# Gate and up products of the FFN: two of eight k-tile pairs by Strassen's scheme, with eight PSUM banks

## The reference, cut to what matters

```
x = x + mixer(rmsnorm(x))
h = rmsnorm(x, ffn_norm[i])
x = x + (silu(h @ w_gate[i]) * (h @ w_up[i])) @ w_down[i]
```

## Time and profile before

| | |
|---|---|
| median of 3 runs | 2175.33 us (2174.98 to 2175.91) |
| the profiled execution | 2175.17 us, span 2173.3 us |
| TensorE busy / weight loads | 2158.6 us (99%) / 1796.3 us (83%) |
| VectorE busy | 1162.3 us (53%) |
| ScalarE busy | 979.9 us (45%) |
| DMA moved | 401.57 MB, mean 185 GB/s |
| slots of the two FFN first halves | 2 x 11 x 16 = 352 of 748 |

### The profile page before, as it was taken

How to read it: one execution, slowest core, us unless ns; L and a number is a source line. 1 busy time by engine, 2 the same in 40 slices (tenths; PEclk the granted TensorE clock), 3 DMA queues, 4 the chain that set the end, 5 groups by cost and what they waited for, 6 DMA issues and landing times.

```text
span 2173.3 us, 27329 instructions
## 1 busy us (share of the span) xinstructions
PE 2158.6 (99%) x10026; PEld 1796.3 (83%) x10026; DVE 1162.3 (53%) x1216; ACT 979.9 (45%) x1125; POOL 15.4 (1%) x14
## 2 busy tenths in 40 slices
PE   8999999999999999999999999999999999999999
PEld 7888888888888888888888888888888888888887
DVE  6887755455444554444455555554445445444443
ACT  5465645444444444444444444554444444443332
POOL 0001000000000000000000000000000000000000
PEclk9999999999999999999999999999999999999999
DMA  7545366666666666656666666566666666666665
GB/s 230 158 142 148 117 188 184 193 190 187 189 191 187 191 185 191 190 189 194 193 185 192 185 187 190 184 186 192 190 188 189 187 192 189 187 188 192 193 194 162
DMA packets 234759, 401.57 MB, mean 185 GB/s; under 512 B 15040, under 2 KB 56128, under 8 KB 234688
## 3 DMA queue, kind: packets, MB, share of 16 engines
q1 hardware_dynamic: 233824, 399.30, 61.9%
q10 hardware_dynamic: 864, 1.30, 0.2%
HBM read 398.45 MB, written 2.10 MB: 184 GB/s over the span
## 4 chain that ended last, share of the span: by engine, by line
PE 98%; DVE 1%; ACT 0%; DMA 0%; issue 0%; SPq 0%; ACTq 0%; DVEq 0%
PE ps L433 29%; PE ps L432 28%; PE ps L431 28%; PE ps L402 6%; PE ps L407 3%; PE ps L465 2%; PE ps L581 0%; PE ps L519 0%; PE ps L590 0%; PE ps L571 0%; DMA res<-in_x 0%; DVE w_lo L1041 0%; PE ps L599 0%; PE ps L507 0%; PE ps L601 0%
## 5 line engine op out<-in xcount | busy, mean ns | idle before, releaser
L1041 DVE TENSOR_TENSOR w_lo<-stage,w_hi 128x1024 fp32r<-128x1024 f32 x748 | 914.6, 1225 | 948.3 <-ACT w_hi L757 948.2
L757 ACT ACTIVATE w_hi<-stage 128x1024 fp32r<-128x1024 f32 x748 | 791.5, 1060 | 1115.7 <-PE ps L433 1063.7
L431 PE MATMUL ps<-w_hi,xs 128*128 128x512 f32 x1792 | 699.7, 390 | 0.0
L433 PE MATMUL ps<-w_hi,xs 128*128 128x512 f32 x1792 | 697.5, 389 | 0.0
L432 PE MATMUL ps<-w_lo,xs 128*128 128x512 f32 x1792 | 697.4, 389 | 0.0
L433 PEld LDWEIGHTS ps<-w_hi,xs 128*128 128x128 f32 x1792 | 336.3, 188 | 69.9
L432 PEld LDWEIGHTS ps<-w_lo,xs 128*128 128x128 f32 x1792 | 336.5, 188 | 69.1
L431 PEld LDWEIGHTS ps<-w_hi,xs 128*128 128x128 f32 x1792 | 336.4, 188 | 69.0
L431 PE MATMUL ps<-w_hi,hs 128*128 128x512 f32 x960 | 375.5, 391 | 0.0
L433 PE MATMUL ps<-w_hi,hs 128*128 128x512 f32 x960 | 373.7, 389 | 0.0
L432 PE MATMUL ps<-w_lo,hs 128*128 128x512 f32 x960 | 373.5, 389 | 0.0
(11 more groups left out here) (131 smaller groups left out, 596.0 us busy)
## 6 DMA issues: line engine op xcount, KB each, us to landing
stage<-in_w_gate SPq DMA_DIRECT2D x176, 512.0 KB, 3.6
stage<-in_w_up SPq DMA_DIRECT2D x176, 512.0 KB, 3.6
stage<-in_w_down SPq DMA_DIRECT2D x176, 512.0 KB, 3.6
stage<-in_conv_w_in SPq DMA_DIRECT2D x96, 512.0 KB, 3.9
stage<-in_attn_w_in SPq DMA_DIRECT2D x48, 512.0 KB, 3.8
stage<-in_attn_w_out SPq DMA_DIRECT2D x32, 512.0 KB, 3.9
stage<-in_conv_w_out SPq DMA_DIRECT2D x32, 512.0 KB, 3.8
stage<-in_attn_w_in SPq DMA_DIRECT2D x32, 256.0 KB, 3.2
```

What stands on the lines that cost most here:

```text
L431: pe.matmul(bank, hi, w_hi[:, slot, cols], start=k == 0, stop=False)
L433: mm = pe.matmul(bank, lo, w_hi[:, slot, cols], start=False, stop=k == tiles - 1)
L757: nc.scalar.activation(w_hi[:, j % RING, :], stage[:, j % RING, :], ACT.Copy).then_inc(hi_done, 1)
L1041: tt(w_lo[:, p, :], stage[:, p, :], f32(w_hi[:, p, :]), ALU.subtract).then_inc(lo_done, 1)
```

## The change

In each FFN block the k-tile pairs 3 and 6 of 8 (k-tiles 6, 7 and 12, 13) are "mixed": for a pair, the two halves of the tokens and the two k-tiles make a 2 x 2 matrix A of activations, the two k-tiles and {gate, up} a 2 x 2 matrix B of weights, and A x B is made by the Strassen-Winograd scheme from 7 products of blocks in place of 8. The float32 sums of weights (T2, T3, T4 and the difference in place of b12) are made by VectorE for each pair, rounded by ScalarE and completed by VectorE into `t_hi` and `t_lo`; those of activations are made once for a layer, in `sx`. The other six pairs are computed as before. Gate and up slots now alternate. Eight accumulators fill the eight banks; they are P1 to P8, in banks 0, 2, 4, 3, 1, 6, 7, 5. Behind a block VectorE adds them up by eight instructions behind its slots 0, 1 and 2 of the next block, with P1 taken out by ScalarE. P6 and P7 share banks 6 and 7 with the turned rows.

TensorE's part:

```diff
+            def plain_pair(n, kp, bank_free):
+                ends = kp == KT // 2 - 1
+                for side, products in enumerate((((P2, lambda k: x_half(k, 0)), (P4, lambda k: x_half(k, 1))),
+                                                 ((P3, lambda k: x_half(k, 0)), (P8, lambda k: x_half(k, 1))))):
+                    slot = (2 * kp + side) % RING
+                    pe.wait_ge(lo_done, n + 2 * kp + side + 1)
+                    for bank, x_of in products:
+                        if kp == 0:
+                            bank_free(bank)
+                        for kk in range(2):
+                            mm = product(bank, x_of(2 * kp + kk), *half_slot(slot, kk),
+                                         kp == 0 and kk == 0, ends and kk == 1)
+                    mm.then_inc(slot_used, 1)
+            def mixed_pair(n, kp, units, bank_free):
...
+                pe.wait_ge(lo_done, n + 2 * kp + 1)
+                product(P1, x_half(k1, 0), *half_slot(g, 0), first, last)
+                product(P2, x_half(k2, 0), *half_slot(g, 1), False, False).then_inc(slot_used, 1)
+                pe.wait_ge(lo_done, n + 2 * kp + 2)
+                product(P3, x_mixed(s, 2), *half_slot(u, 1), False, False)
+                product(P5, x_mixed(s, 0), *half_slot(u, 0), first, last).then_inc(slot_used, 1)
+                pe.wait_ge(t_ready, 2 * units + s + 1)
+                product(P6, x_mixed(s, 1), t_hi[:, 1, :], t_lo[:, 1, :], first, last)
+                product(P4, x_half(k2, 1), t_hi[:, 2, :], t_lo[:, 2, :], False, False)
+                product(P7, x_mixed(s, 3), t_hi[:, 0, :], t_lo[:, 0, :], first, last).then_inc(t_used, 1)
...
+                    for kp in range(KT // 2):
+                        if kp in MIXED_PAIRS:
+                            mixed_pair(n, kp, units, bank_free)
+                        else:
+                            plain_pair(n, kp, bank_free)
+                        if kp == 1:
+                            if first_time:
+                                turn_res(q, 3)
+                            else:
+                                turn_hidden(units - 1)
```

ScalarE's part: 

```diff
+            def mixed_high(count):
+                act.wait_ge(t_step, 3 * count + 3)
+                nc.scalar.activation(t_hi[:, :, :], t_raw[:, :, :], ACT.Copy).then_inc(t_high, 1)
...
+                def unit_steps(i):
+                    return {0: [lambda: take_p1(done + i, n)], 2: [lambda: silu(done + i, q)],
+                            5: [lambda: hidden_high(done + i, i)]}
+                def unit(i, steps):
+                    for j in range(16):
+                        s = MIXED_PAIRS.index(j // 2) if j // 2 in MIXED_PAIRS else None
+                        count = None if s is None else 2 * (done + i) + s
+                        split(first, 1, 16, i, j, None if s is None or j % 2 == 0 else count + 1)
+                        if s is not None and j % 2:
+                            mixed_high(count)
+                        for step in steps.get(j, ()):
+                            step()
```

VectorE's part:

```diff
+            def take_mixed(units):
+                dve.wait_ge(t_used, 2 * units + 2)
+                dve.wait_ge(p1_taken, units + 1)
+                add_in(act_rows[:, 0, :], P6, gate_rows[:, 0, :], at + 1)
+                add_in(act_rows[:, 1, :], P7, act_rows[:, 0, :], at + 2)
+                add_in(act_rows[:, 0, :], P5, act_rows[:, 0, :], at + 3)
+            def take_gate(units, n):
+                dve.wait_ge(slot_used, n + KT - 1)
+                add_in(gate_rows[:, 0, :], P2, gate_rows[:, 0, :], at + 4)
+                add_in(gate_rows[:, 1, :], P4, act_rows[:, 1, :], at + 5)
+                add_in(act_rows[:, 1, :], P5, act_rows[:, 1, :], at + 6)
+            def take_up(units, n):
+                dve.wait_ge(slot_used, n + KT)
+                add_in(act_rows[:, 0, :], P3, act_rows[:, 0, :], at + 7)
+                add_in(act_rows[:, 1, :], P8, act_rows[:, 1, :], at + 8)
+            def mix_weights(first, i, j, count):
+                for jj in (j, j + 1):
+                    dve.wait_ge(loaded[jj % RING], 16 * ((first + jj) // RING + 1) + 64 * i)
+                dve.wait_ge(t_used, count)
+                tt(t3, b22, b12, ALU.subtract).then_inc(t_step, 1)
+                tt(b12, b12, b11, ALU.subtract).then_inc(t_first, 1)
+                dve.wait_ge(t_first, count + 1)
+                tt(t2, b22, b12, ALU.subtract).then_inc(t_step, 1)
+                dve.wait_ge(t_step, 3 * count + 2)
+                tt(t4, b21, t2, ALU.subtract).then_inc(t_step, 1)
+            def mixed_low(count):
+                dve.wait_ge(t_high, count + 1)
+                tt(t_lo[:, :, :], t_raw[:, :, :], f32(t_hi[:, :, :]), ALU.subtract).then_inc(t_ready, 1)
...
+                    return {0: [lambda: take_mixed(done + i)], 1: [lambda: take_gate(done + i, n)],
+                            2: [lambda: take_up(done + i, n)], 3: [lambda: hid(done + i, q)],
+                            5: [lambda: hidden_low(done + i, i)]}
+                def unit(i, steps):
+                    for j in range(16):
+                        if s is not None and j % 2 == 0:
+                            mix_weights(first, i, j, count)
+                        split(first, 1, 16, i, j)
+                        if s is not None and j % 2:
+                            mixed_low(count)
+                        for step in steps.get(j, ()):
+                            step()
```

More of the change, by code:

```diff
@@ L86, in trunk @@
         mat = sb("mat", [P, 2, P])
-        cross = sb("cross", [P, 4, TOK])
         total = sb("total", [P, 4, TOK])
[L89 to L93, removed]
+        rows_part = ExitStack()
+        gated = sb("gated", [P, 4, TOK], stack=rows_part)
+        colsum = sb("colsum", [P, TOK], stack=rows_part)
+        rstd = sb("rstd", [P, TOK], stack=rows_part)
+        rows_part.close()
+        raw_part = ExitStack()
+        t_raw = sb("t_raw", [P, 3, WIDE], stack=raw_part)
+        raw_part.close()
+        sb("gated_colsum_rstd", [P, 3, WIDE])
+        before_ffn = ExitStack()
+        cross = sb("cross", [P, 4, TOK], stack=before_ffn)
+        square = sb("square", [P, 4, TOK], stack=before_ffn)
+        sums = sb("sums", [P, 4, TOK], stack=before_ffn)
+        before_ffn.close()
+        in_ffn = ExitStack()
+        t_hi = sb("t_hi", [P, 3, WIDE], F32R, stack=in_ffn)
+        t_lo = sb("t_lo", [P, 3, WIDE], F32R, stack=in_ffn)
+        in_ffn.close()
+        sb("cross_square_sums", [P, 3, 4 * TOK])
         eps = sb("eps", [P, 2])
@@ L150, in trunk @@
         ytap, y_full = square, sums
+        scaled = total
+        mixed = gated[:, 0:2, :].rearrange("p a (b t) -> p (a b) t", b=2)
         def f32(ap):
@@ L354, in load_ffn @@
             def load_ffn(first, layer):
-                with sp.Fori(0, FT // 4) as i:
-                    load_block(first + 16 * i, w_gate[layer], 0, WIDE * i, WIDE, KT)
-                    load_block(first + 16 * i + 8, w_up[layer], 0, WIDE * i, WIDE, KT)
+                with sp.Fori(0, BLOCKS) as i:
+                    for s in range(KT // 2):
+                        rows2 = slice(2 * s * P, 2 * (s + 1) * P)
+                        for side, w in enumerate((w_gate[layer], w_up[layer])):
+                            j = 2 * s + side
+                            load(first + 16 * i + j, j % RING, w[rows2, :][:, bass.ds(WIDE * i, WIDE)], WIDE)
             load_wide(S_AO, attn_w_out, KT)
@@ L647, in turn_hidden, with product @@
                 pe.wait_ge(hid_made, 2 * blocks + 2)
-                pe.wait_ge(hidden_ready, blocks)
-                turn_rows(act_rows, TURN_BANK).then_inc(hid_turned, 1)
+                turn_rows(act_rows, FFN_TURN).then_inc(hid_turned, 1)
+            def product(bank, x_of, b_hi, b_lo, start, stop):
+                hi, lo = x_of
+                pe.matmul(ps[:, bank, :], hi, b_hi, start=start, stop=False)
+                pe.matmul(ps[:, bank, :], hi, b_lo, start=False, stop=False)
+                return pe.matmul(ps[:, bank, :], lo, b_hi, start=False, stop=stop)
@@ new lines, in x_half, with x_mixed, half_slot @@
+            def x_half(k, a):
+                return xs[:, k, a * P:(a + 1) * P], xs[:, k, TOK + a * P:TOK + (a + 1) * P]
+            def x_mixed(s, form):
+                return sx[:, s, form, 0:P], sx[:, s, form, P:TOK]
+            def half_slot(slot, kk):
+                cols = slice(kk * WIDE, (kk + 1) * WIDE)
+                return w_hi[:, slot, cols], w_lo[:, slot, cols]
+            def plain_pair(n, kp, bank_free):
[11 more added lines that the diff above has]
+                    mm.then_inc(slot_used, 1)
@@ new lines, in mixed_pair @@
+            def mixed_pair(n, kp, units, bank_free):
+                s = MIXED_PAIRS.index(kp)
+                first, last = s == 0, s == len(MIXED_PAIRS) - 1
+                k1, k2 = 2 * kp, 2 * kp + 1
+                g, u = 2 * kp % RING, (2 * kp + 1) % RING
+                if first:
```

(23 more changed lines are left out.)

184 lines of the change are left out of this document (138 added, 46 removed).

## The result

The changed kernel takes 2180.8 us (2179.45 to 2182.38, 9 runs) against 2175.12 us before: a ratio of 1.0027, 95% interval 1.0016 to 1.0037. It is slower by 5.7 us, where 2165.5 us and a gain were forecast, with 2156 to 2183 as the range.

A forecast was written before the change was run, and what follows sets the result against it. TensorE, busy 99% of the span, was taken as the bound. Removed matmuls -29.9, late place +19.0, block 0 +1.0 and down projection +0.2 gave -9.7 us, so 2165.5 us, range 2156 to 2183.

The forecast's parts named there:

- The saving, 29.9 us: 132 TensorE matmuls of 0.2267 us removed, two mixed pairs in each of 22 blocks; a steady block falls by 1.36 us.
- The late place: Slots 5 to 7, blocks 1 to 10: TensorE waits for helpers after the transposes, 0.95 us a block, 19.0 us given back.
- rival B: VectorE's register work for nine waits between turn and 1536 subtraction lies open: 1.8 us a block, 2182 us; 14%.
- The duration of what was added: Per block, VectorE's sums, evicting adds and subtractions take 14.5 us, ScalarE's roundings and eviction 3.6 us.
- What else could be late, and is not.: Evictions, second pair, loads and activation mixing: nearly all hidden, with 0.2 us for the down projection and 1.0 for block 0.
- The covers: Spare time before the next block wants freed accumulators P2, P3 and P8: 1.4, 0.9 and 1.6 us, none used.
- C: Rival: evicting adds behind a block use up their spare time, half a microsecond a block, gain gone, 2175 us; 7%.
- Block 0: In each layer activation and weight mixing share slots, slot 12 about 0.4 us late; 0.5 us each, 1.0 in all.
- The down projection's start: It starts with P1 and P5; P5 is free at 5.5 us against 5.44 wanted: 0.1 us each, 0.2 in all.
- rival D: TensorE's clock falls after each stop, three slow matmuls behind it: 0.6 us a block, 12 us, 2178 us; 3%.
- The decision point: The wait per block, over 20 blocks, from which the saving is lost: (29.9 - 1.2) / 20 = 1.43 us.
- the forecast's own range: The range for the main forecast alone, 2159 to 2172 us, from 0.7 to 1.3 us of wait a block; 68%.

The follow-up runs named there:

- e1: The changed kernel with the transposes of the hidden rows behind slot 2 again instead of slot 3 (blocks 1 to 10): 2150.9 us, ratio 0.9885 to the kernel before.
- e2: The changed kernel, transposes left behind slot 3, with VectorE's four weight sums of the first mixed pair ahead of its subtraction on the hidden rows: 2150.5 us, ratio 0.9886.
- e7: The changed kernel with the transposes behind slot 2 and one 128x2 Silu in block 0 of each layer: 2148.8 us, ratio 0.9880.
- e4: The changed kernel with one 128x2 Silu, output not used, on ScalarE in block 0 of each layer: 2176.8 us, ratio 1.0006 to the kernel before.
- e3: The changed kernel with VectorE's loop over blocks 1 to 10 written out: 2174.75 us, ratio 0.9998 to the kernel before.
- e8: The changed kernel with transposes behind slot 2, the 128x2 Silu in block 0 and VectorE's loop written out: 2149.0 us, ratio 0.9879.

## Why the prediction was wrong, point by point

- **The saving, 29.9 us.** The count was right (9894). Per block the floor is 43.20 in e1, e2 and e7, so 1.23 us and not 1.36: about 2.8 us of the 29.9 are not had, in the matmuls on the summed weights and just behind them.
- **The late place.** Right in place and in kind: slots 5 to 7 of blocks 1 to 10, TensorE waiting for the split of slot 6, 20 times, with the queue order as the cause. e1 and e2 take it away by two routes. This is the step that failed, by its size: "I take 0.95 a block". It is 44.60 - 43.20 = 1.40 (e4 against e7), 28 us and not 19.0. Of the missing 0.45, 0.23 is the register work between ScalarE's rounding and the subtraction (e3), a part of rival B that I priced but did not put into the forecast. 0.12 is the start of ScalarE 1.19 behind the first transpose and not 1.07. I had taken that hand-over from the earlier trace rows, an instruction with a fixed address; outside the loop this one comes at 1.07 too, so register work is the likely cause here as well, though no run wrote ScalarE's loop out. The last 0.10 is at TensorE: it loses 0.10 at its restart (0.33 between the first two starts), some 0.04 in the next matmuls and 0.06 in front of the summed weights, where the forecast had 0.10 for the last of these and nothing for the others. These are read in the timeline and were not tried by themselves.
- **The duration of what was added.** The 128x1536 subtraction takes 1.75 (1.76 forecast), the rounding 1.49 (1.49), the sums 0.69, chained starts 0.03 apart: right. The own waits cost what the earlier trace rows said: 722.12 + 0.69 to 722.84 is 0.03, while the free start at 722.12 comes 0.08 ahead of its predecessor's end. The Trainium skill (VectorE: DVE Perf Modes, The DRAIN you can't avoid) says that chained operations take the same time with a semaphore after each as with one at the end. The trace does not agree for a sum that waits for the one before it: it starts 0.72 behind that one (722.12 to 722.84), a free one 0.60 (721.52 to 722.12).
- **"What else could be late, and is not."** This step failed too, for the evictions: a term put at nothing was 4.0 us (e4). The covers were counted with ScalarE's queue free of table loads, and I had not asked which table the loop is entered with. C had the place but not the cause.
- **Block 0** cost 0.6 us in layer 0 (0.4 in e8) and nothing in layer 1, where 0.5 each was taken: from the last transposes of block 0 to those of block 1, with the slot by which they stand apart put right, e7 has 43.77 and 43.18. The down projection's start cost 0.42 and not 0.1. The projections ahead of the FFNs, the convolution and the last projection keep their times.
- **The clock (rival D)** stayed at its full level: the mean granted clock of the profiled execution is 0.999, with a stop of about 1.04 us in each of 20 blocks.

The sum by measured terms: -29.9 + 2.8 + 28.0 + 4.0 + 0.6 + 0.8 = +6.3, against +5.7 measured. The profiled spans have +5.7 too; in them the chain up to the last transposes is 6.9 later, and from there to the end of the span it is 1.2 shorter (235.50 against 236.72), all of it behind the last matmul. Why, no run here shows.

The late place (9.0 us more than forecast), the table loads (4.0) and the saving that was not had (2.8) are what turned a forecast of -9.7 into a loss.

The forecast said faster with 63%. The decision point was named, 1.43 a block; the measured 1.40 of the late place and 0.13 of the matmuls are together over it, and the table loads come on top. That the time still fell into the stated range is owed to the range's width, since it took in most of rival B: the forecast's own range ended at 2172. The mistake was to leave so little between 0.95 and 1.43 and to add up a chain of ten short instructions over three engines with the smallest hand-over at each.

## What to carry to other kernels

When work is taken off the bounding engine, draw up the queue order of the helpers at the one place where they must wait for a result of that engine, and count from there to the next thing the bounding engine wants; the helpers' shares (67% and 51%) told nothing. An instruction in that row that waits and has an address worked out in the loop is to be priced with its register work (here 0.11 us on ScalarE and 0.23 us on VectorE). A step that waits belongs behind the work that doesn't need it, or its cause one slot earlier: either edit turned a loss of 5.7 us into a gain of 24 to 25. When an activation function moves across the head of a loop, look with which table the loop is entered.

## What the runs showed of the hardware that I had not expected

- In a loop, a VectorE instruction with a computed address that waited for ScalarE started 0.26 us after the end of what it waited for; with the loop written out, 0.03 us. Where nobody waited for it, it cost nothing (2148.8 and 2149.0). A ScalarE instruction of this kind that waited for TensorE started 0.15 us after the end in the loop and 0.04 us outside it.
- Behind a stop of 1.04 us TensorE's first two 128x512 matmuls start 0.33 apart, the rest 0.23, at full clock. The length of the stop is not what does it: behind a stop of 0.14 us (709.24 to 709.61, 0.37 between starts) the next two start 0.33 apart too (709.61, 709.94).
- A table load of 1.28 us stood twice in each pass of a loop that uses Silu and Copy when the loop was entered behind a square root, and in no pass when a 128x2 Silu came before it.
- Matmuls moving the summed weights start 0.233 us apart, and so do the three behind them; those moving the ring's start 0.227 apart in a steady row and 0.232 in the first six behind a stop. The cause is open.
